# A state space mixer regrouped: sixteen scans over 512 time steps become four batches of scans over 128 block states

## The reference, cut to what matters

```python
A_bar = jnp.exp(A * dt)
B_bar = ((A_bar - 1.0) / A)[..., None] * Bm
Bu = jnp.einsum('blgc,gnc->blgn', uf.astype(jnp.complex64), B_bar)
a = jnp.broadcast_to(A_bar, Bu.shape)
_, states = lax.associative_scan(_linear_recurrence_op, (a, Bu), axis=1)
y = jnp.einsum('blgn,gcn->blgc', states, Cm).real
y = y + d_skip.astype(jnp.float32).reshape(S5_GROUPS, S5_GROUP) * uf
y = jax.nn.gelu(y.reshape(bsz, L, S5_WIDTH))
```

## Time and profile before

| | |
|---|---|
| time, median of 3 runs | 2410.23 us (2408.67 to 2410.54) |
| profiled execution, first to last instruction | 2409.5 us |
| PE busy | 2333.4 us (97%) |
| DVE busy | 1213.0 us (50%) |
| ACT busy | 766.0 us (32%) |
| POOL busy | 226.4 us (9%) |

### The profile page before, as it was taken

One profiled execution on the slowest core, in us unless ns is written; L12 is line 12 of the kernel. 1 busy time (PEld: TensorE's weight loads), 2 busy tenths in 40 slices (PEclk: granted clock), 3 DMA queues, 4 the chain that ended last, 5 costly groups with the idle time before them and its releaser, 6 DMA issues.

```text
span 2409.5 us, 26555 instructions
## 1 busy us (share of the span) xinstructions
PE 2333.4 (97%) x10176; PEld 1873.3 (78%) x10176; DVE 1213.0 (50%) x1287; ACT 766.0 (32%) x774; POOL 226.4 (9%) x174
## 2 busy tenths in 40 slices
PE   8987989999999999999999999999999999999996
PEld 6754667887888888888888888888888888888884
DVE  6899984455336444334444434444434444436444
ACT  5311215444225333223333223333222222226432
POOL 3366560400000000000000000000000000000001
PEclk9998999999999999999999999999999999999997
DMA  5111111213322222222222223222222222232221
GB/s 220 70 48 60 53 70 71 75 53 114 127 108 87 104 98 82 91 95 104 104 90 91 85 100 104 104 87 94 84 101 104 104 87 94 84 110 105 91 101 70
DMA packets 37383, 224.39 MB, mean 93 GB/s; under 512 B 4289, under 2 KB 4801, under 8 KB 17121
## 3 DMA queue, kind: packets, MB, share of 16 engines
q1 hardware_dynamic: 37344, 223.88, 26.2%
HBM read 219.67 MB, written 4.19 MB: 93 GB/s over the span
## 4 chain that ended last, share of the span: by engine, by line
PE 91%; DVE 6%; issue 1%; POOL 0%; ACT 0%; DMA 0%; DVEq 0%; SPq 0%; POOLq 0%; ACTq 0%
PE bank L432 29%; PE bank L433 29%; PE bank L434 29%; DVE w_lo L1050 1%; PE bank L523 1%; PE bank L468 0%; PE bank L508 0%; DVE xs_lo L1071 0%; DVE QKV L1143 0%; DVE QKV L1144 0%; PE bank L603 0%; DVE Y L1459 0%; PE bank L509 0%; DVE QKV L1141 0%; DVE QKV L1142 0%
## 5 line engine op out<-in xcount | busy, mean ns | idle before, releaser
L432 PE MATMUL bank<-xs_hi,w_hi 128*128 128x512 f32 x2432 | 957.7, 394 | 11.8 <-DVE w_lo L1057 10.4
L433 PE MATMUL bank<-xs_lo,w_hi 128*128 128x512 f32 x2432 | 949.2, 390 | 0.0
L434 PE MATMUL bank<-xs_hi,w_lo 128*128 128x512 f32 x2432 | 949.2, 390 | 0.0
L765 ACT ACTIVATE w_hi<-w_raw 128x2048 fp32r<-128x2048 f32 (+1 forms) x214 | 375.1, 1753 | 867.4 <-PE bank L434 859.6
L1050 DVE TENSOR_TENSOR w_lo<-w_raw,w_hi 128x2048 fp32r<-128x2048 f32 (+1 forms) x216 | 461.9, 2139 | 185.2 <-ACT w_hi L765 182.2
L432 PEld LDWEIGHTS bank<-xs_hi,w_hi 128*128 128x128 f32 x2432 | 457.9, 188 | 118.5 <-issue 11.9
L433 PEld LDWEIGHTS bank<-xs_lo,w_hi 128*128 128x128 f32 x2432 | 457.9, 188 | 96.0 <-issue 2.6
L434 PEld LDWEIGHTS bank<-xs_hi,w_lo 128*128 128x128 f32 x2432 | 457.7, 188 | 95.6
L432 PE MATMUL bank<-mid_hi,w_hi 128*128 128x512 f32 x704 | 278.4, 395 | 0.0
L434 PE MATMUL bank<-mid_hi,w_lo 128*128 128x512 f32 x704 | 278.4, 395 | 0.0
L433 PE MATMUL bank<-mid_lo,w_hi 128*128 128x512 f32 x704 | 278.4, 395 | 0.0
(11 more groups left out here) (235 smaller groups left out, 1519.7 us busy)
## 6 DMA issues: line engine op xcount, KB each, us to landing
w_raw<-in_w_up SPq DMA_DIRECT2D x88, 1024.0 KB, 4.8
w_raw<-in_w_down SPq DMA_DIRECT2D x64, 704.0 KB, 4.0
w_raw<-in_w_in SPq DMA_DIRECT2D x32, 1024.0 KB, 4.8
w_raw<-in_w_out SPq DMA_DIRECT2D x16, 1024.0 KB, 4.8
w_raw<-in_w_pg SPq DMA_DIRECT2D x16, 1024.0 KB, 4.8
x_res<-in_x SPq DMA_DIRECT2D x8, 512.0 KB, 5.6
out_h<-Y SPq DMA_DIRECT2D x16, 256.0 KB, 2.3
Y<-in_x SPq DMA_DIRECT2D x2, 1280.0 KB, 12.3
```

Of the source, the lines that this page charges most:

```text
L432: nc.tensor.matmul(out, w_h, x_h, start=first, stop=False)
L433: nc.tensor.matmul(out, w_h, x_l, start=False, stop=False)
L434: return nc.tensor.matmul(out, w_l, x_h, start=False, stop=last)
L765: nc.scalar.activation(w_hi[c % 2][:, 0:width], w_raw[c % 2][:, 0:width], ACT.Copy).then_inc(hi_made, 1)
```

## The change

The recurrence is taken four steps at a time (`STEPS` = 4, `BLOCKS` = 128). With x_b the state ahead of block b, x_{b+1} = A_bar^4 x_b + (sum over the four inputs of a block of A_bar^(3-s) B_bar u), and the four outputs of a block are C A_bar^k x_b plus a lower triangular 4 x 4 arrangement of C A_bar^d B_bar that acts on the block's own inputs. So:

- POOL builds on the chip, for four pairs at a time (a batch, `S5_BATCHES` = 4), the matrix that drives the block states (`make_push`), the one that reads them (`make_read`), and the angles of the 128 block states of four pairs in one row of 512 (`find_turns`, which was DVE's). `first_powers` makes A_bar to A_bar^4 in `s5_constants`.
- PE transposes the push matrices (`turn_push`), multiplies B and the read matrices into the within-block matrix (`spread_intra`), makes the drive of the block states (`drive_states`) and reads (`read_states`), all in float32 with 128 columns. ACT copies these matrices out of PSUM (`keep_drive`, `keep_intra`, `keep_y`).
- DVE's `rotate_scan` works on four pairs at once, with scans of 128 elements, and now rotates forward too. POOL's six forward rotations per pair are gone, and so are `u_half`, `u_rest`, `turn_b` and `bu`.
- The input u must lie with (step, channel) on the partitions: DVE writes it step by step in `evacuate(0)` to `evacuate(3)`, SP writes it to DRAM and reads it back in the other order (`u_to_blocks`, `blocks_in`, ahead of the loads of slots 7 and 8), and y goes back by the same way (`y_from_blocks`, `y_rows_in`). `add_skip` waits for that, and the GELU moves to slot 18.

Batch c is in slots 5 + 2c (`turn_push`, `trig`), 6 + 2c (`spread_intra`, `drive_states`, `rotate_scan`), 8 + 2c (`read_states`) and 10 + 2c (`add_skip`). The diff, cut to its core (most removed lines are those of the functions printed above, and are left out):

```diff
+S5_BATCHES = 4
+PER_BATCH = PAIRS // S5_BATCHES
+STEPS = 4
+BLOCKS = SEQ // STEPS
+TURN_SLOT = 5
+DRIVE_SLOT = 6
+READ_SLOT = 8
+SKIP_SLOT = 10
+GELU_SLOT = 18
...
+            def u_to_blocks(c):
+                sp.wait_ge(evacuated, c + 1)
+                for j in range(PER_BATCH):
+                    rows = slice(32 * j, 32 * j + 32)
+                    sp.dma_start(u_dram[c, j].rearrange("s r n -> r s n"),
+                                 Y[rows, c, :].rearrange("r (s n) -> r s n", s=STEPS)).then_inc(u_out, 16)
+            def blocks_in(c):
+                sp.dma_start(U4[:, c, :].rearrange("p (j n) -> p j n", j=PER_BATCH),
+                             u_dram[c].rearrange("j s r n -> (s r) j n")).then_inc(u_in[c], 16)
+            def y_from_blocks(c):
+                sp.wait_ge(y_blocks_made, c + 1)
+                sp.dma_start(y_dram[c].rearrange("j s r n -> (s r) j n"), y_blocks[:]).then_inc(y_out, 16)
+            def y_rows_in(c):
+                sp.wait_ge(y_out, 16 * (c + 1))
+                for j in range(PER_BATCH):
+                    rows = slice(32 * j, 32 * j + 32)
+                    sp.dma_start(y_back[rows, c, :].rearrange("r (s n) -> r s n", s=STEPS),
+                                 y_dram[c, j].rearrange("s r n -> r s n")).then_inc(y_in[c], 16)
...
+            def turn_push(c):
+                pe.wait_ge(push_made, c + 1)
+                if c:
+                    pe.wait_ge(drive_made, c)
+                for z in range(2):
+                    for i in range(PER_BATCH):
+                        js = slice(i * P, (i + 1) * P)
+                        t = nc.tensor.transpose(bank[4 + z][:, js], push[z][:, js], ident[:])
+                t.then_inc(push_turned, 1)
+            def spread_intra(c):
+                pe.wait_ge(read_made, c + 1)
+                if c:
+                    pe.wait_ge(intra_made, c)
+                for i in range(PER_BATCH):
+                    js = slice(i * P, (i + 1) * P)
+                    for z in range(2):
+                        m = nc.tensor.matmul(bank[6][:, js], B_times[z][:, js], Q[c % 2][:, z, i, 0:STEPS, :].rearrange("p d r -> p (d r)"),
+                                             start=z == 0, stop=z == 1)
+                m.then_inc(intra_spread, 1)
+            def drive_states(c):
+                pe.wait_ge(drive_made, c + 1)
+                pe.wait_ge(u_in[c], 16)
...
+                if c:
+                    pe.wait_ge(states_made, c)
+                for z in range(2):
+                    for i in range(PER_BATCH):
+                        js = slice(i * P, (i + 1) * P)
+                        m = nc.tensor.matmul(bank[2 + z][:, js], drive[z][:, i, :], U4[:, c, js], start=True, stop=True)
+                m.then_inc(driven, 1)
+            def read_states(c):
+                pe.wait_ge(states_made, c + 1)
+                pe.wait_ge(intra_made, c + 1)
+                if c:
+                    pe.wait_ge(y_blocks_made, c)
+                for i in range(PER_BATCH):
+                    out = bank[7][:, i * P:(i + 1) * P]
+                    nc.tensor.matmul(out, intra[:, i, :], U4[:, c, i * P:(i + 1) * P], start=True, stop=False)
+                    for z in range(2):
+                        m = nc.tensor.matmul(out, Q[c % 2][:, z, i, 1:STEPS + 1, :].rearrange("p d r -> p (d r)"),
+                                             state[z][:, i, 0:BLOCKS], start=False, stop=z == 1)
+                m.then_inc(states_read, 1)
...
-                if n == 3:
-                    turn_b()
-                if READ_SLOT <= n < READ_SLOT + PAIRS:
-                    read_states(n - READ_SLOT)
-                if BU_SLOT <= n < BU_SLOT + PAIRS:
-                    bu(n - BU_SLOT)
+                for c in range(S5_BATCHES):
+                    if n == TURN_SLOT + 2 * c:
+                        turn_push(c)
+                    if n == READ_SLOT + 2 * c:
+                        read_states(c)
+                for c in range(S5_BATCHES):
+                    if n == DRIVE_SLOT + 2 * c:
+                        spread_intra(c)
+                        drive_states(c)
...
+            def trig(c):
+                act.wait_ge(turns_made, c + 1)
+                if c:
+                    act.wait_ge(states_made, c)
+                else:
                     act.wait_ge(tile_done, 1)
+                nc.scalar.activation(sin_t, turns, ACT.Sin, scale=SIN_SCALE)
+                link(nc.scalar.activation(cos_t, turns, ACT.Sin, scale=math.pi))
+                nc.scalar.activation(cos_t, cos_t, ACT.Square).then_inc(trig_made, 1)
...
+                if n == N_Q:
+                    dve.wait_ge(bbar_made, 1)
+                if n == N_V:
+                    dve.wait_ge(push_turned, S5_BATCHES)
+                    dve.wait_ge(intra_spread, S5_BATCHES)
+                if n < N_G:
                     dst = QKV[:, n - N_Q, :]
...
+                link(tt(pr, b_im, sin, ALU.mult))
+                link(tt(re, re, pr, ALU.add))
+                link(tt(pr, b_re, sin, ALU.mult))
+                link(tt(im, im, pr, ALU.subtract))
+                for i in range(PER_BATCH):
+                    size = s5s[:, 17, PER_BATCH * c + i:PER_BATCH * c + i + 1].to_broadcast([P, BLOCKS])
+                    for part in (re, im):
+                        last = nc.vector.tensor_tensor_scan(part[:, i, :], size, part[:, i, :], 0.0, ALU.mult, ALU.add)
+                link(last)
+                tt(b_re, im, sin, ALU.mult)
+                link(tt(b_im, re, sin, ALU.mult))
+                tt(re, re, cos, ALU.mult)
+                link(tt(im, im, cos, ALU.mult))
+                tt(re, re, b_re, ALU.subtract)
+                tt(im, im, b_im, ALU.add).then_inc(states_made, 1)
             def add_skip(c):
...
+                dve.wait_ge(y_in[c], 64)
...
-                if BU_SLOT <= n < BU_SLOT + PAIRS:
+                for c in range(S5_BATCHES):
+                    if n == DRIVE_SLOT + 2 * c:
+                        rotate_scan(c)
+                    if n == SKIP_SLOT + 2 * c:
+                        add_skip(c)
...
+            def find_turns(c):
...
+                if c == 0:
+                    pool.wait_ge(sq_used, KT)
+                else:
+                    pool.wait_ge(trig_made, c)
+                link(tt(n, at, whole, ALU.mult))
+                link(ts(n, n, TO_INT, None, ALU.add))
+                link(ts(n, n, TO_INT, None, ALU.subtract))
+                link(tt(t, at, high, ALU.mult))
+                link(tt(t, t, n, ALU.subtract))
+                link(tt(n, at, low, ALU.mult))
+                link(tt(t, t, n, ALU.add))
+                ts(t, t, 0.5, -0.5, ALU.min, ALU.max).then_inc(turns_made, 1)
...
+            def make_push(c):
...
+                if c:
+                    pool.wait_ge(push_turned, c)
+                tt(out[0], b[0], a[0], ALU.mult)
+                link(tt(t, b[1], a[1], ALU.mult))
+                link(tt(out[0], out[0], t, ALU.subtract))
+                tt(out[1], b[0], a[1], ALU.mult)
+                link(tt(t, b[1], a[0], ALU.mult))
+                tt(out[1], out[1], t, ALU.add).then_inc(push_made, 1)
...
+                if c:
+                    pool.wait_ge(intra_spread, c)
+                for z in range(2):
+                    m = nc.gpsimd.tensor_copy(B_times[z].rearrange("p (i s r) -> p i s r", s=STEPS, r=32), b[z])
+                link(m)
...
+            def make_read(c):
...
+                if c >= 2:
+                    pool.wait_ge(states_read, c - 1)
...
+                tt(out[0], m[0], a[0], ALU.mult)
+                link(tt(t, m[1], a[1], ALU.mult))
+                link(tt(out[0], out[0], t, ALU.add))
+                tt(out[1], m[1], a[0], ALU.mult)
+                link(tt(t, m[0], a[1], ALU.mult))
+                tt(out[1], out[1], t, ALU.subtract).then_inc(read_made, 1)
...
+            for c in range(S5_BATCHES):
+                find_turns(c)
+                make_push(c)
+                make_read(c)
```

## The result

The changed kernel takes 2335.39 us (median, 2334.78 to 2336.4) against 2410.39 beside it: ratio 0.9685, interval 0.9673 to 0.9697, 75.0 us less. Predicted were 2350 us in a range of 2325 to 2388. The profiled execution has a span of 2333.2 us.

The account below looks back on a forecast made before the run. DVE was taken to bound slots 4 to 21; with POOL the new pace at 34.8 us per batch, tile 22 starts at 304.3, 60.7 us earlier: 2409.5 - 60.7 = 2348.8, given as 2350 us, range 2325 to 2388.

Parts of the forecast that it names:

- PE sets the pace: Rival, chance 0.17: POOL's B is 29.5 us or less, tile 22 starts at 281.7 to 286, 2327 to 2331 us.
- the four rivals: PE sets the pace, The lock costs in full, DVE sets the pace, and POOL too slow to win anything (0.07).
- The floor of PE: Start of tile 22 if PE never waited: 281.7 us, 83.3 us earlier than before the change.
- B: POOL's time per batch, predicted 34.8 us against 29.5 us of PE, so POOL would set the pace.
- POOL alone: POOL's instructions, copies and gaps of one batch without DVE's interference, predicted 27.7 us.
- POOL beside DVE: What DVE adds per batch: w_lo 2.06 us twice, fifteen short instructions about 0.2 us each.
- Start and first batch: POOL starts the batches at 61.1; batch 0 meets three w_lo and takes 33.9 us, read_made at 95.0.
- PE waiting 5 to 9 us in each batch: Sign of a right forecast: PE waits that long for POOL ahead of L533 or L543, not for DVE.
- The lock costs in full: Rival, chance 0.20: each SBUF-only DVE instruction adds its length to POOL, 39.2 to 43 us per batch, 2368 to 2383 us.
- DVE sets the pace: Rival, chance 0.08: rotation over 30 us makes states_made late for PE's read; at 35 us of rotation, 2365 us.
- What was costed at nothing: u and y through DRAM: u at 98, wanted at 97, bounds 0 and 2 us; late y covered by DVE's slack.
- the clock: Sign of a wrong forecast: PE's granted clock falls in the waits and costs in the stretch behind 200.

Follow-up runs that it names:

- e2: Changed kernel with four more 512-column POOL instructions behind the angles of each batch; 2357.04 us, ratio 0.9769.
- e3: Changed kernel with the angles of batches 1 to 3 left out on POOL, those of batch 0 used again; 2326.19 us, ratio 0.9644.
- e5: Changed kernel with POOL's order per batch made push matrices, angles, read matrices; 2340.21 us, ratio 0.9706.
- e8: Changed kernel without DVE's 32 scans over the block states; 2334.87 us, ratio 0.9682.
- e4: Changed kernel without the way of u and y through DRAM; 2338.71 us, ratio 0.9694.
- e6: Changed kernel with the skip term one slot later (SKIP_SLOT 11 for 10); 2338.85 us, ratio 0.9696.
- e10: Changed kernel with the two B_times copies moved from POOL to ACT and POOL's order push matrices, read matrices, angles; 2329.95 us, ratio 0.9659.
- e11: e10 with the skip term one slot later (SKIP_SLOT 11); 2327.45 us, ratio 0.965.
- e1: Changed kernel with POOL's order per batch made push matrices, read matrices, then angles; 2333.52 us, ratio 0.9675.
- e12: The changed kernel itself, run again on the same chip as e11; 2335.88 us, ratio 0.9685.
- e9: Changed kernel with the two B_times copies moved from POOL to ACT, POOL's order unchanged; 2336.03 us, ratio 0.9687.
- e7: Changed kernel with the edits of e5 and e6 together: angles between push and read matrices, skip term one slot later; 2339.55 us, ratio 0.9704.

## Why it came out so

**The side and the mechanism were right.** DVE set the pace and no longer does; POOL sets it now, as the forecast said; e2 and e3 show it from both sides. But it does so by less than 2 us per batch, and the time came out 15 us under the forecast, near the rival "PE sets the pace". The range took in the times of three of the four rivals, so that the time lies in it says little about the mechanism; the traces do. The floor of PE was right within 2 us: in e3, L606 starts at 291.68, less its wait of 0.92 us and the 11.1 us of tile 22, so 279.7 against 281.7.

**The step that was mis-sized is B.** `read_made` of batch 3 was put at 199.4, and POOL's last instruction ends at 185.6: 13.8 us too late, which is all but 0.7 us of the error at tile 22 (304.3 against 289.8) and of the error in the end. It splits so:
- *POOL alone.* Predicted 27.7 us per batch. The shortest duration of each line, summed over a batch, is 24.5, with 1.0 of gaps 25.5. The two 512 copies take 1.17 together, not 2.0. The third tensor-scalar, with two constants as limits, takes 0.62, not the 1.49 of the earlier trace rows. Gaps are 1.0, not 1.3. One line, L1694, meets DVE in all four batches of the changed kernel and is never under 1.50 there; alone it takes 1.05 (e5, where it is L1696):
```profile
85.53 1.05 POOL L1696 TENSOR_TENSOR QKV<-QKV,powers 128x512 f32<-128x512 f32 x1
```
- *POOL beside DVE.* Predicted 7.1 us (two `w_lo` at 2.06, fifteen short ones at 0.2). The excess over the durations alone is 6.0, 5.9 and 5.2 us in batches 1 to 3. One instruction per batch is held nearly for the whole of a `w_lo` (3.25 against 1.28, had 3.34), which costs 1.9 to 2.0. In batches 1 and 2 a second one (2.17 and 2.08 against 1.04) starts when the `w_lo` is half done and costs 1.1 and 1.0; batch 3 has no second one. The rest is 2.9, 2.9 and 3.3 us, in pieces of up to 0.5 us (one of 0.8): the 3 us predicted for the short ones were right, the `w_lo` term (4.1 us against 3.1, 3.0 and 2.0) was too large.
- *Start and first batch.* Predicted 61.1 and 33.9 us; they were 60.15 and 31.8. The three `w_lo` of the first batch cost 6.2 us, as predicted; the difference is POOL alone.

By batch that is 0.95 for the start and 2.1 + 3.2 + 3.4 + 4.1 us for the four, together 13.8 us; 2.2 us in each is POOL alone.

**PE waiting 5 to 9 us in each batch** was wrong with it: at B = 31.4 against PE's 29.5 it is 1.9 us per batch, and 6.8 us were seen in all four together.

**"The lock costs in full"** is ruled out: the short instructions, which that rival charged with their whole length of 6.9 us, cost POOL 2.9 to 3.3 us of a batch, and the scans, charged with 2.4, some 0.5 (e8). The two engines don't lose alike: DVE's eight scans grow by 5.2 us (7.87 against 2.63). Why POOL loses so little to them, no run shows. **"PE sets the pace"** was nearly true in time (2335 against its 2327 to 2331), not in mechanism. **"DVE sets the pace"** (rotation over 30 us) fell with 22.0 us; 25 and 12 were predicted, 22.0 and 11.2 seen.

**What was costed at nothing.** u was in time, and by far: SP issues the last reads of it by 71.6 us, they take 3.7 us (median) to land, and PE wants u at 94.75; the prediction had u at 98. y was not in time, by 3.58 and 4.29 us. Its way out is not what is late: it is issued at 129.33 and takes 5.5 us (median). Its way back stands on SP behind a load of weights, and that load waits until `w_lo` is done (on DVE at 153.69), here just ahead of the skip term (timeline of SP):
```profile
153.72 0.33 SPq L373 DMA_DIRECT2D w_raw<-in_w_in  x1
154.09 1.86 SPq L394 DMA_DIRECT2D Y<-y_blocks_out  x4
```
The four issues take 1.86 us and land 4.7 us (median) after each, so y is there near 160, and DVE asks for it at 156.2. It costs nothing in the changed kernel, because PE waits for POOL anyway (e4 and e6 gain nothing). In e10, where that cover is gone, DVE still waits 0.85 us for y and spends 1.62 us on the skip term ahead of the rotation of batch 2; e11 moves both behind it and is 2.5 us faster (the ranges of the runs lie apart, though the intervals of the ratios overlap). How much of the 2.5 is y's alone, no run separates.

**What goes with the waits is the clock**, which the prediction had named as a way to be wrong. e5 and e6 missed first by waits that they did not expect (10.4 and 9.2 us in sum), and then by this. The granted level falls from 2.4 to 1.2 GHz in or behind some of the waits. The changed kernel after its wait of 3.30 us (windows, then the timeline of PE):
```profile
112.00:114.00 2.00, 2.00 (x7) 1.54 (x5) 1.97 (x3) 1.08 (x2) 1.94 (x4) 0.50 0.00 0
114.00:116.00 2.00, 2.00 (x8) 1.62 (x7) 1.97 (x3) 0.00 (x0) 2.00 (x2) 0.70 0.00 0
```
```profile
112.72 0.63 PE L483 MATMUL bank<-xs_hi,w_lo 128*128 128x512 f32 x1
113.14 0.63 PE L481 MATMUL bank<-xs_hi,w_hi 128*128 128x512 f32 x1
```
The matmuls come 0.43 us apart in place of 0.23 until 115, so nearly half of each microsecond at the lower level is lost. The granted clock of each trace, in windows of 2 us, gives how long it was at 1.2 GHz. Time at that level inside a wait costs nothing; the column below has what lies outside of the waits.

What a wait costs can be read from two places on PE: where it stands when it first comes to the transposes of batch 0, ahead of any wait there (80.40 in e3), and the start of the instruction behind tile 22 (L606, or its line in the other kernels). From the first to the second, less the waits over 0.3 us, e3 takes 291.68 - 0.92 - 80.40 = 210.36 us, with the clock at 1.00 throughout. "Beyond" is what the others take more:

| kernel | waits, us | longest | at the transposes, us | L606, us | beyond the waits | at 1.2 GHz outside the waits, us |
|---|---|---|---|---|---|---|
| e3 | 0.92 | 0.92 | 80.40 | 291.68 | 0 | 0 |
| e11 | 1.19 | 1.19 | 80.75 | 292.47 | 0.17 | 0 |
| e10 | 2.75 | 2.75 | 79.60 | 294.30 | 1.59 | 2.9 |
| e1 | 5.96 | 4.04 | 80.55 | 298.86 | 1.99 | 3.2 |
| changed | 6.83 | 3.30 | 80.80 | 300.96 | 2.97 | 3.4 |
| e12 (changed again) | 6.91 | 3.29 | 80.02 | 302.35 | 5.06 | 9.2 |
| e9 | 7.57 | 2.76 | 79.87 | 300.25 | 2.45 | 3.2 |
| e8 | 7.63 | 6.47 | 79.92 | 300.98 | 3.07 | 6.1 |
| e7 | 9.10 | 6.19 | 79.88 | 303.06 | 3.72 | 6.9 |
| e6 | 9.19 | 3.70 | 81.11 | 306.25 | 5.59 | 9.5 |
| e4 | 9.19 | 3.29 | 80.15 | 304.94 | 5.24 | 9.1 |
| e5 | 10.43 | 5.63 | 79.78 | 305.44 | 4.87 | 9.1 |
| e2 | 22.58 | 6.95 | 80.27 | 322.15 | 8.94 | 17.0 |

Half of the last column accounts for the one before it within 0.9 us, but for the changed kernel, where 1.3 us are left. It also tells why e5, with the longer waits and more time at 1.2 GHz in all (13.7 us against 10.2), loses no more than e6: 4.5 us of it lie inside e5's waits, 0.7 inside e6's. In the changed kernel waits come to 6.8 us, what goes with them to 3.0, and PE is 0.4 us later at the transposes. That is 9.3 us over e3's own 0.9, and e3 gained 9.2.

The length of a wait does not decide alone whether the clock falls. The changed kernel run again (e12) has nearly the same waits, yet its clock stays down longer after the first long one, and falls a second time behind one of 1.88 us:
```profile
174.00:176.00 2.00, 1.58 (x9) 1.54 (x10) 2.00 (x4) 0.56 (x1) 1.88 (x4) 0.69 0.00 0
176.00:178.00 2.00, 2.00 (x6) 0.78 (x5) 1.97 (x4) 1.08 (x2) 2.00 (x4) 0.50 0.00 0
```
It does not fall behind the wait of 1.92 us in e1 or that of 2.34 in e9. So e9's theory, a wait over about 3 us, is not borne out. What decides stays open, and with it differences of a few microseconds between two executions.

## What to carry to other kernels

- Where one engine works without a break against another that interrupts it now and then, cost it by its durations alone, plus what is left of each long instruction when its next one starts (here 2.0 us in full, 1.0 to 1.1 in half), and some 3 us for all the short ones of a batch together (here 15, of 7 us alone). Here copies and clamps were cheaper than the nearest arithmetic row of the same size (0.59 and 0.62 us against 1.04 and 1.49).
- When the slack is down to 2 us per batch, moving one product forward only makes the next one late (e1, e5). The gain came when three small things went together: less work on the pacing engine, the order by due time, and the skip term with its late transfer moved off the path (e11).
- Count more than the length of a matmul engine's waits: where they came to 5 us and more here, they cost 1.3 to 1.7 times their sum, and two executions of the same kernel differed by 2 us in it.

## What was not expected of the hardware

A GpSimd copy of 512 columns takes 0.6 us, and a tensor-scalar with minimum and maximum 0.62, against 1.50 for those that add a constant. Beside GpSimd a VectorE scan of 128 columns takes three times as long (0.98 against 0.33), while GpSimd loses some 0.5 us to eight of them. VectorE's products with one operand in PSUM lose nothing: they take 0.68 us in both cases (L1247, L1248 and L1262), where those with both in SBUF go from 0.69 to as much as 1.78 (L1260). The granted clock of TensorE fell behind a wait of 1.88 us in one execution and not behind one of 2.34 in another.
